# Five dense matmuls a slice instead of six, with a second partial sum in PSUM that is joined at eviction

## The chip, the cores and the metric

The kernel runs on one core of one Trainium2 chip. The metric is the device time of one execution in microseconds (us), median of several. TensorE (PE) multiplies, VectorE (DVE), ScalarE (ACT) and GpSimd (POOL) work elementwise, and SyncE (SP) issues the weight loads. Matmul results land in PSUM, eight banks of 512 fp32 columns per partition; all else that is on the chip lies in SBUF.

## The reference

One inference step of a two-layer recurrent decoder, in fp32, for one prompt of 512 tokens and eight sample sequences of 4 tokens, which share the weights: T = 544 tokens in all. D_MODEL is 2048. Cut to what matters:

```
layer 0: u = rmsnorm(h) @ ab_w_in     -> DeltaNet heads and GLA heads -> y
layer 1: u = rmsnorm(h) @ cd_w_in     -> SSD heads and RG-LRU channels -> y
h = h + y @ (ab_w_out | cd_w_out)
h = h + sigmoid(rmsnorm(h) @ ple_w_gate) * (p @ ple_w_proj)
```

Six large products with the 544 tokens: into `ab` (57 tiles of 128 output columns), `out0` (16), `gate0` (16), `cd` (37), `out1` (16), `gate1` (16), 158 tiles together.

## The kernel before, in words

Activations stand transposed: the 2048 model columns lie on 16 groups of 128 partitions, tokens along the free axis. A *slice* is one 128x128 block of weights times the 544 tokens; a *tile* is 16 slices, whose sum is 128 output columns for all tokens. There are 158 x 16 = 2528 slices.

To reach fp32 accuracy with the fp32r format each operand is split in two: x = xh + xl and w = w_hi + w_lo. A slice is three products, w_hi.xh, w_lo.xh and w_hi.xl, each over two halves of 272 tokens (`HALF`), since one matmul writes one PSUM bank: six matmuls of 272 columns (line 582). All three products add into the same columns. Each of them loads its stationary block first.

Weights come in *quarters* of four slices. SP loads a quarter into `w_raw` (six buffers), ACT copies it to `w_hi` (`split_hi`, line 1136), DVE subtracts to get `w_lo` (`split_lo`, line 1683), and PE waits for `lo_ready`. The dense tiles alternate between two PSUM buffers, `psd[0]` and `psd[1]`, of two banks each; tile d may begin when tile d-2 has been evicted (`dense_read`).

Between dense slices PE does the small *work groups* of the branches (into `psw`, also two buffers); a written plan (`target`, `FILL`, `LEAD`) says after which dense slice each group is issued. Each engine has a function `fill(to)` that does its share of the dense work up to slice `to`: on ACT the w_hi copies, on DVE the evictions and the w_lo subtractions. The branches' own steps on ACT and DVE stand between the calls of `fill`, in program order. A group waits for the reader of the group two before it and for its own inputs.

Evictions, all on DVE, each over 544 columns from `D0` = 240 on: for `ab` and `cd` tiles `evacuate(d)` multiplies by the row scale `rstd` (line 1708); in the `out` stages h is added (line 2350); in the `gate` stages line 2377 multiplies by `rstd`, ACT takes the sigmoid (1522), and DVE multiplies by the projection and adds into h (2388, 2390). At a stage's last tile (`last_tile`) ACT and DVE already make xh (`hi_part`, line 1205) and xl (`lo_part`, line 1745) for the next stage's *head* tile, whose slices wait for them one by one. POOL sums squares for the norm (line 2590), and PE adds them up over partitions in a norm group (lines 604 and 605).

## Time and profile before

| | |
|---|---|
| median of 3 runs | 2451.63 us (2447.52 to 2455.24) |
| span of the profiled execution, first to last instruction | 2447.1 us |
| the profiled execution's own time | not listed apart; the runs lie 0.4 to 8.1 us above the span |
| PE busy | 2384.2 us (97%), 21567 matmuls |
| dense matmuls (line 582) | 15168 of them |
| DVE / ACT / POOL busy | 52% / 39% / 15% |
| DMA | 111 GB/s on average |
| mean granted TensorE clock | 0.993 of full |

Matmuls overlap in the records: one of 272 columns is recorded with some 290 ns, but the next one starts 125 ns after it. For the cost of a matmul the distance from start to start is to be read, not the duration. The page's idle times are what is left when nothing of an engine is recorded as running.

### The profile page before, as it was taken

The numbers are of one execution on the slowest core, as the hardware profiler recorded it, in microseconds if no ns is written. First come the engines' busy times: TensorE is split into PE (matmuls) and PEld (weight loads), VectorE is DVE, ScalarE is ACT, GpSimd is POOL, SyncE is SP. The second block draws the span as 40 slices with busy tenths as digits, with TensorE's granted clock in tenths as the row PEclk, the third lists the DMA queues.
The fourth block names the chain that finished last, engine by engine and source line by source line (L and its number), as shares of the span: only waits on it lengthen the run. The fifth ranks groups of instructions, "written<-read, shape, count | busy, mean of one in ns | idle before, by whom it ended". The sixth has DMA issues, their size and how long they took to land.

```text
span 2447.1 us, 50327 instructions
## 1 busy us (share of the span) xinstructions
PE 2384.2 (97%) x21567; PEld 2273.9 (93%) x21567; DVE 1280.8 (52%) x2387; ACT 958.4 (39%) x1547; POOL 373.5 (15%) x558
## 2 busy tenths in 40 slices
PE   7999999999999999999999999999999999999996
PEld 7998999988999999899999999988899999999996
DVE  6655656565654564622444465566656663243432
ACT  5523444323444344432332353443355553243332
POOL 3101101111101101111111212122212211111111
PEclk9999999999999999999999999999999999999998
DMA  9433333333344454552233343233323354223232
GB/s 232 115 103 107 116 98 116 108 90 106 108 121 117 136 152 122 194 161 87 87 97 109 110 114 92 70 89 87 86 80 103 95 190 127 87 83 96 79 88 76
DMA packets 375535, 271.16 MB, mean 111 GB/s; under 512 B 24419, under 2 KB 346733, under 8 KB 374800
## 3 DMA queue, kind: packets, MB, share of 16 engines
q1 hardware_dynamic: 341424, 172.53, 26.0%
q0 software_dynamic: 22080, 72.77, 9.3%
q10 hardware_dynamic: 11808, 22.63, 2.6%
q8 instruction: 171, 2.80, 0.5%
q14 instruction: 52, 0.43, 0.1%
HBM read 220.24 MB, written 48.37 MB: 110 GB/s over the span
## 4 chain that ended last, share of the span: by engine, by line
PE 86%; DVE 6%; ACT 5%; issue 2%; DMA 1%; POOL 0%; ACTq 0%; DVEq 0%; POOLq 0%
PE psd L582 71%; PE psw L605 2%; PE psw L604 2%; PE psw L632 1%; PE psw L682 1%; DVE arena L1967 1%; PE psw L660 1%; PE psw L668 1%; ACT w_hi L1136 1%; DVE w_lo L1683 1%; PE psw L674 0%; PE psw L646 0%; PE psw L654 0%; PE psw L971 0%; PE psw L1066 0%
## 5 line engine op out<-in xcount | busy, mean ns | idle before, releaser
L582 PE MATMUL psd<-xh,w_hi 128*128 128x272 f32 x5056 | 1098.3, 298 | 8.9 <-DVE w_lo L1683 5.3
L582 PE MATMUL psd<-xl,w_hi 128*128 128x272 f32 x5056 | 1048.4, 289 | 2.9 <-DVE xl L1745 2.1
L582 PE MATMUL psd<-xh,w_lo 128*128 128x272 f32 x5056 | 1045.2, 288 | 0.0
L582 PEld LDWEIGHTS psd<-xh,w_hi 128*128 128x128 f32 x5056 | 795.0, 189 | 60.0 <-issue 40.5
L582 PEld LDWEIGHTS psd<-xh,w_lo 128*128 128x128 f32 x5056 | 796.4, 189 | 0.0
L582 PEld LDWEIGHTS psd<-xl,w_hi 128*128 128x128 f32 x5056 | 792.2, 189 | 4.2 <-DVE xl L1745 3.1
L1683 DVE TENSOR_TENSOR w_lo<-w_raw,w_hi 128x512 fp32r<-128x512 f32 x632 | 433.7, 706 | 380.5 <-ACT w_hi L1136 379.4
L1136 ACT CAST w_hi<-w_raw 128x512 fp32r<-128x512 f32 x632 | 376.7, 616 | 573.2 <-PE psd L582 499.3
L2590 POOL TENSOR_TENSOR states<-states,extra 128x544 f32<-128x544 f32 x59 | 86.7, 1469 | 514.4 <-ACT extra L1191 514.3
L2377 DVE TENSOR_TENSOR extra<-psd,rstd 128x544 f32<-128x544 f32 x32 | 23.2, 724 | 156.0 <-PE psd L582 138.9
L2350 DVE TENSOR_TENSOR arena<-arena,psd 128x544 f32<-128x544 f32 x32 | 23.1, 721 | 136.7 <-PE psd L582 129.9
L1792 DVE SCALAR_TENSOR_TENSOR arena<-raws,pv,arena 128x511 f32<-128x511 f32 (+2 forms) x120 | 86.2, 748 | 2.0
L1522 ACT ACTIVATE extra<-extra 128x544 f32<-128x544 f32 x32 | 21.1, 660 | 135.2 <-DVE extra L2377 135.2
L2512 POOL DMA_DIRECT2D raws<-uT_scratch x27 | 18.7, 692 | 347.8 <-DMA uT_scratch<-mix 323.0
L2525 POOL COPY smp<-hist 128x24 f32<-128x24 f32 x44 | 15.7, 357 | 277.5 <-DVE raws L1708 233.7
L1708 DVE TENSOR_TENSOR mix<-psd,rstd 128x544 f32<-128x544 f32 x55 | 39.3, 715 | 26.9 <-PE psd L582 23.5
L1708 DVE TENSOR_TENSOR raws<-psd,rstd 128x544 f32<-128x544 f32 x39 | 28.1, 721 | 43.0 <-PE psd L582 42.7
L605 PE MATMUL psw<-rawsR,mixR 128*128 128x288 f32 x192 | 49.4, 294 | 0.0
L604 PE MATMUL psw<-rawsR,mixR 128*128 128x256 f32 x192 | 48.9, 280 | 0.0
L1745 DVE SCALAR_TENSOR_TENSOR xl<-arena,pv,xh 128x544 fp32r<-128x544 f32 x64 | 45.9, 778 | 2.6 <-ACT xh L1205 2.5
L2618 POOL DMA_DIRECT2D raws<-in_ple_w_proj_dram x32 | 23.0, 720 | 158.1 <-DVE extra L2388 158.1
L1205 ACT ACTIVATE xh<-arena,pv 128x544 fp32r<-128x544 f32 x64 | 42.5, 739 | 6.6 <-DVE arena L2350 5.0
(514 smaller groups left out, 2376.9 us busy)
## 6 DMA issues: line engine op xcount, KB each, us to landing
w_raw<-in_ab_w_in_dram SPq DMA_DIRECT2D x224, 256.0 KB, 3.0
w_raw<-in_cd_w_in_dram SPq DMA_DIRECT2D x148, 256.0 KB, 3.0
w_raw<-in_ple_w_gate_dram SPq DMA_DIRECT2D x128, 256.0 KB, 3.1
w_raw<-in_ab_w_out_dram SPq DMA_DIRECT2D x64, 256.0 KB, 2.8
w_raw<-in_cd_w_out_dram SPq DMA_DIRECT2D x64, 256.0 KB, 2.8
uT_scratch<-mix ACTq DMA_DIRECT2D x53, 272.0 KB, 2.2
hT_scratch<-arena POOLq DMA_DIRECT2D x8, 1088.0 KB, 6.4
arena<-hT_scratch POOLq DMA_DIRECT2D x8, 1088.0 KB, 9.5
```

Of the source, the lines that this page charges most:

```text
L582: mm = pe.matmul(out[:, D0 + HALF * half:D0 + HALF * (half + 1)], w[:, r, k % QH, :], x[:, k, HALF * half:HALF * (half + 1)], start=(k == ...
L604: pe.matmul(W[:, SEQ - CUT:SEQ], lhsT, rhs[:, 0:CUT], **kw)
L605: return pe.matmul(W[:, SEQ:SEQ + T - CUT], lhsT, rhs[:, CUT:T], **kw)
L632: mm = pe.matmul(W[rows, c], lhsT(t, j), rhs[rows, c], start=True, stop=True)
L660: pe.transpose(W[:, P * t:P * t + P], src[:, P * t:P * t + P], ident[:, :])
L1136: act.copy(w_hi[:, q % NW], w_raw[:, q % NW]).then_inc(S["hi_ready"], 1)
L1205: act.mul(xh[:, c, :], hT(c), src[:, c:c + 1]).then_inc(S["x_hi"], 1)
L1683: dve.tensor_tensor(w_lo[:, q % NW], w_raw[:, q % NW], w_hi[:, q % NW].bitcast(F32), ALU.subtract).then_inc(S["lo_ready"], 1)
L1708: dve.tensor_tensor(dst, psd[d % 2][:, D0:D0 + T], rstd[:, :], ALU.mult)\
L1745: dve.scalar_tensor_tensor(xl[:, c, :], hT(c), src[:, c:c + 1], xh[:, c, :].bitcast(F32), ALU.mult, ALU.subtract).then_inc(S["x_ready"], 1)
L1792: go(dve.scalar_tensor_tensor(y, x, w, y, ALU.mult, ALU.add))
L2590: pool.tensor_tensor(acc, acc, extra[:, T * (2 + c % 2):T * (3 + c % 2)], ALU.add)\
```

## The change

The six matmuls of a slice become five. The first 288 tokens (`NA`) have three, w_hi.xh, w_lo.xh and w_hi.xl, in the tile's first bank. The other 256 (`NBK`) have two: one matmul of 512 columns with w_hi, whose moving operand is 256 columns of xh followed by the same 256 columns of xl, and one of 256 columns, w_lo.xh. The 512-column one fills the whole second bank with two sums: columns 512 to 767 hold w_hi.xh + w_lo.xh, columns 768 to 1023 hold w_hi.xl. To make that operand possible xh and xl become one tensor `xhl`, with a slice's xh row and xl row one behind the other.

At eviction the two sums are joined. For `ab`, `cd` and `gate` tiles (126 of them) ACT waits for the tile's end and copies the second sum to SBUF (`copy_low`, 128x256), and DVE adds it to the first in place (`join`) before it evicts as before. For the 32 `out` tiles DVE adds 544 columns into h and then, in a second instruction that waits for the first, the 256 of the second sum. At a head tile PE waits for `x_ready` after two matmuls of the slice instead of after four. `D0` is 224.

```diff
-        xh, xl = sb("xh", [P, KT, T], F32R), sb("xl", [P, KT, T], F32R)
+        xhl = sb("xhl", [P, KT, 2, T], F32R)
+        xh, xl = xhl[:, :, 0, :], xhl[:, :, 1, :]
...
-                out = psd[d % 2]
-                for i, (w, x) in enumerate(((w_hi, xh), (w_lo, xh), (w_hi, xl))):
-                    if head and i == 2:
-                        pe.wait_ge(S["x_ready"], KT * ph + k + 1)
-                    for half in range(2):
-                        mm = pe.matmul(out[:, D0 + HALF * half:D0 + HALF * (half + 1)], w[:, r, k % QH, :],
-                                       x[:, k, HALF * half:HALF * (half + 1)],
-                                       start=(k == 0 and i == 0), stop=(k == KT - 1 and i == 2))
-                mm.then_inc(S["slice_done"], 1)
+                hi, lo = w_hi[:, r, k % QH, :], w_lo[:, r, k % QH, :]
+                own, both = psd[d % 2][:, D0:SEQ], psd[d % 2][:, SEQ:2 * SEQ]
+                pe.matmul(own, hi, xhl[:, k, 0, 0:NA], start=k == 0, stop=False)
+                pe.matmul(own, lo, xhl[:, k, 0, 0:NA], start=False, stop=False)
+                if head:
+                    pe.wait_ge(S["x_ready"], KT * ph + k + 1)
+                pe.matmul(own, hi, xhl[:, k, 1, 0:NA], start=False, stop=k == KT - 1)
+                pe.matmul(both.rearrange("p (i t) -> p i t", i=2), hi, xhl[:, k, :, NA:T], start=k == 0, stop=False)
+                pe.matmul(both[:, 0:NBK], lo, xhl[:, k, 0, NA:T], start=False, stop=k == KT - 1)\
+                    .then_inc(S["slice_done"], 1)
...
+            def copy_low(d):
+
+                lows[0] = d + 1
+                if d in LOW:
+                    act.wait_ge(S["slice_done"], tile_end(d))
+                    if d >= 2:
+                        act.wait_ge(S[f"dense_read{d % 2}"], d // 2)
+                    act.copy(low[:, d % 2], psd[d % 2][:, SEQ + NBK:SEQ + 2 * NBK]).then_inc(S["low_copied"], 1)
... (ACT fill)
+                    if n % SL == 0 and lows[0] < n // SL:
+                        copy_low(n // SL - 1)
                     for q in SPLITS.get(n, []):
                         split_hi(q)
...
+                if to % SL == 0 and lows[0] < to // SL and TILES[to // SL - 1][3] in ("gate0", "gate1"):
+                    copy_low(to // SL - 1)
...
+            def join(d):
+
+                late = psd[d % 2][:, SEQ:2 * SEQ]
+                dve.wait_ge(S["slice_done"], tile_end(d))
+                dve.wait_ge(S["low_copied"], LOW[d] + 1)
+                link(dve.tensor_tensor(late[:, 0:NBK], late[:, 0:NBK], low[:, d % 2], ALU.add))
... (evacuate; the same in gate)
-                dve.wait_ge(S["slice_done"], tile_end(d))
+                join(d)
... (out_proj)
-                    dve.tensor_tensor(hT(c), hT(c), psd[d % 2][:, D0:D0 + T], ALU.add)\
+                    link(dve.tensor_tensor(hT(c), hT(c), psd[d % 2][:, D0:D0 + T], ALU.add))
+                    dve.tensor_tensor(hT(c)[:, NA:T], hT(c)[:, NA:T], psd[d % 2][:, SEQ + NBK:SEQ + 2 * NBK], ALU.add)\
                        .then_inc(S[f"dense_read{d % 2}"], 1)
```

## Rows read from the trace of the kernel before

**Rows 1.** The page's part 1, and PE and its granted clock in part 2
```profile
PE 2384.2 (97%) x21567; PEld 2273.9 (93%) x21567; DVE 1280.8 (52%) x2387; ACT 958.4 (39%) x1547; POOL 373.5 (15%) x558
...
PE   7999999999999999999999999999999999999996
...
PEclk9999999999999999999999999999999999999998
```

**Rows 2.** The page's part 4: the chain that ended last, by engine
```profile
PE 86%; DVE 6%; ACT 5%; issue 2%; DMA 1%; POOL 0%; ACTq 0%; DVEq 0%; POOLq 0%
```

**Rows 3.** PE's waits: waiting line, releaser: total us, places, longest; 25 rows
```profile
PE psw L1066 <- DMA ident<-in_cf_dram: 6.4, 1, 6.4
...
PE psw L610 <- ACT raws L1335: 0.2, 1, 0.2
```

**Rows 4.** PE's timeline in gate0: start us, us recorded, instruction, count
```profile
1364.79 0.41 PE L582 MATMUL psd<-xl,w_hi 128*128 128x272 f32 x2
...
1371.55 0.42 PE L582 MATMUL psd<-xl,w_hi 128*128 128x272 f32 x2
1371.80 0.28 PE L604 MATMUL psw<-rawsR,mixR 128*128 128x256 f32 x1
...
1373.28 0.41 PE L582 MATMUL psd<-xh,w_hi 128*128 128x272 f32 x2
```

**Rows 5.** Groups of PE by form: xcount | busy us, mean ns | idle before
```profile
L605 PE MATMUL psw<-rawsR,mixR 128*128 128x288 f32 x192 | 49.4, 294 | 0.0
L604 PE MATMUL psw<-rawsR,mixR 128*128 128x256 f32 x192 | 48.9, 280 | 0.0
...
L668 PE MATMUL psw<-states,arena 128*32 128x256 f32 x128 | 8.6, 385 | 0.0
...
L668 PE MATMUL psw<-states,arena 128*32 128x512 f32 x32 | 4.3, 604 | 0.0
```

**Rows 6.** Groups of DVE by form
```profile
L1683 DVE TENSOR_TENSOR w_lo<-w_raw,w_hi 128x512 fp32r<-128x512 f32 x632 | 433.7, 706 | 380.5 <-ACT w_hi L1136 379.4
...
L2350 DVE TENSOR_TENSOR arena<-arena,psd 128x544 f32<-128x544 f32 x32 | 23.1, 721 | 136.7 <-PE psd L582 129.9 <-DMA arena<-hT_scratch 6.8
...
L2124 DVE TENSOR_TENSOR arena<-raws,arena 128x256 f32<-128x256 f32 x20 | 8.3, 416 | 0.0
```

**Rows 7.** Groups of ACT by form: a copy of 256 columns out of PSUM
```profile
L1410 ACT COPY extra<-psw 128x256 f32<-128x256 f32 x8 | 3.0, 375 | 62.6 <-PE psw L668 62.6
```

**Rows 8.** All engines' waits: evictions of ab and cd tiles
```profile
DVE raws L1708 <- PE psd L582: 42.7, 18, 6.1
...
DVE mix L1708 <- PE psd L582: 23.5, 10, 4.7
```

**Rows 9.** The timeline at a tile's end in an ab stage, 407 to 412 us
```profile
411.01 1.12 ACT L1136 CAST w_hi<-w_raw 128x512 fp32r<-128x512 f32 x2
...
411.65 1.29 DVE L1683 TENSOR_TENSOR w_lo<-w_raw,w_hi 128x512 fp32r<-128x512 f32 x2 [3.17 <-ACT w_hi L1136]
```

**Rows 10.** The timeline from gate0 to cd
```profile
1436.90 4.59 ACT L1205 ACTIVATE xh<-arena,pv 128x544 fp32r<-128x544 f32 x7
...
1439.17 0.41 PE L582 MATMUL psd<-xl,w_hi 128*128 128x272 f32 x2
...
1439.70 4.95 DVE L1745 SCALAR_TENSOR_TENSOR xl<-arena,pv,xh 128x544 fp32r<-128x544 f32 x7
...
1444.57 0.71 DVE L2377 TENSOR_TENSOR extra<-psd,rstd 128x544 f32<-128x544 f32 x1
...
1448.97 1.48 POOL L2590 TENSOR_TENSOR states<-states,extra 128x544 f32<-128x544 f32 x1 [17.12 <-ACT extra L1191]
...
1452.21 0.59 PE L604 MATMUL psw<-states,ones 128*128 128x256 f32 x2
```

**Rows 11.** The timeline at the start of out0
```profile
1051.74 0.52 PE L582 MATMUL psd<-xh,w_hi 128*128 128x272 f32 x2 [3.14 <-DVE arena L2350]
```

**Rows 12.** The timeline behind the last dense slice
```profile
2419.02 0.72 DVE L2377 TENSOR_TENSOR extra<-psd,rstd 128x544 f32<-128x544 f32 x1 [10.31 <-PE psd L582]
```

More of the change, by code:

```diff
@@ L30 @@
 TAPS = 4
-HALF = T // 2
-D0 = SEQ - HALF
 CUT = SEQ // 2
+NA, NBK = T - CUT, CUT
+D0 = SEQ - NA
 WT = slice(SEQ - CUT, SEQ - CUT + T)
@@ L183 @@
 SEMS = """w_landed0 w_landed1 w_landed2 w_landed3 w_landed4 w_landed5 hi_ready lo_ready slice_done dense_read0 dense_read1 stage_stored0 stage_stored1
-act_chain dve_chain pool_chain work_ready in_copied nrm_sq nrm_ln nrm_rstd x_hi x_ready y_done h_loaded0 h_loaded1 h_loaded2 h_loaded3 z_loaded dn_z gl_z cd_z x_read sq_added sq_summed
+act_chain dve_chain pool_chain low_copied work_ready in_copied nrm_sq nrm_ln nrm_rstd x_hi x_ready y_done h_loaded0 h_loaded1 h_loaded2 h_loaded3 z_loaded dn_z gl_z cd_z x_read sq_added sq_summed
 consts_loaded params_loaded rows_loaded xy_loaded0 xy_loaded1 xy_loaded2 xy_loaded3 xy_loaded4 xy_loaded5 h_stored
@@ L259, in trunk @@
         wa2 = sb("wa2", [P, GLA_KW])
+        low = sb("low", [P, 2, NBK])
         C32 = c32[:, 0:6 * 32].rearrange("p (l j) -> p l j", l=6)
@@ L385, in trunk @@
         POS = {dk: n for n, dk in enumerate(ORDER)}
+        LOW = {d: i for i, d in enumerate(d for d, t in enumerate(TILES) if t[3] not in ("out0", "out1"))}
         def tile_end(d):
@@ L1123, in _ @@
         def _(act):
-            at, chained, stores, split, loaded = [0], [0], [0], [0, 0], [0, 0]
+            at, chained, stores, lows, split, loaded = [0], [0], [0], [0], [0, 0], [0, 0]
             def link(ins):
@@ L1154, in fill @@
                     at[0] += 1
+                if to % SL == 0 and lows[0] < to // SL and TILES[to // SL - 1][3] in ("gate0", "gate1"):
+                    copy_low(to // SL - 1)
+                if to in (end_slice("ab"), end_slice("cd")) and lows[0] < to // SL:
+                    copy_low(to // SL - 1)
                 if to in (end_slice("ab"), end_slice("cd")) and stores[0] < to // SL:
@@ L2368, in gate @@
                         last_tile(3)
-                    dve.wait_ge(S["slice_done"], SL * (d + 1))
+                    join(d)
                     if c == 0:
```

## The prediction

> **What bounds the kernel now.** I read the page's busy shares first, then the chain that ended last, then what PE waited for, then the timeline at the places which the change touches. PE is busy 97% of the span at a granted clock of nine tenths of full or more in every fortieth of the span but the last [rows 1]. The chain that sets the end runs 86% through PE [rows 2]. PE's whole list of waits has 25 rows; they add up to about 39.5 us in 53 places, 6.4 us of it at the very start [rows 3]. So PE's own stream is the bound, and DVE at 52% and ACT at 39% mostly follow it: of the idle time before DVE's w_lo subtractions 379 us end with ACT's w_hi [rows 6]. What counts is the distance from one dense matmul's start to the next.
>
> **The dense stream, the term that gains.** In gate0, 28 rows of two dense matmuls each run from 1364.79 to 1371.80 us, 56 matmuls in 7.01 us, 125.2 ns each [rows 4]. At 2.4 GHz, the upper of the clock's two levels, 272 columns take 113.3 ns. So 11.9 ns of a matmul are over its columns. The question is whether they are fixed per matmul or grow with the columns. Right behind stand twelve fp32r matmuls of 256 and 288 columns by turns: 1.48 us [rows 4] for 3264 columns, which are 1.36 us, so 10 ns each over. Their recorded durations are 280 ns for 256 columns and 294 ns for 288 [rows 5], 14 ns for 32 columns, or 0.44 ns a column; 1/2.4 is 0.417, and the whole distance spread over the columns would be 125.2/272 = 0.460. The row with 512 columns is an fp32 one: 604 ns against 385 for 256 [rows 5], 0.855 ns a column where two passes at full clock are 0.833. That is 2.6% over, not 10.5%. Most of the extra is thus fixed, and a matmul that fills a whole bank shows nothing else that is odd.
>
> The columns stay: 3 x 288 + 512 + 256 = 1632 = 6 x 272. A slice is now 6 x 125.2 = 751 ns, and will be 680 + 5 x 11.9 = 739.5 ns. That saves 11.9 ns x 2528 slices = 30.1 us. With the 10 ns of the mixed stream in the new slice (680 + 50 = 730 ns) it would save 21 ns a slice, 53 us; with the extra wholly proportional to columns, nothing. The 512-column matmul reads its operand as two runs of 256, one row of the tensor apart. No matmul in the trace has such an operand; from below it costs nothing, from above I allow as much as a matmul's whole extra, 12 ns a slice, which would eat the gain. I take nothing, since each of its runs is one of contiguous columns, as every operand in the trace is. So 30 us.
>
> A page of the Trainium skill speaks against so much. "TensorE: Matmul & The Clock Gate", section "Back-to-back issue gap", gives an isolated matmul's distance as the columns at 2.4 GHz and about 2.5 ns; by it the sixth matmul costs 6.3 us in all. The rows above show 10 to 12 ns over the columns where each matmul has its own weight load, so the measurement decides. The same section gives about 131 ns as the sustained distance at 512 columns with weight loads, below the 213 ns of the columns; by that the slice would lose another 94 ns.
>
> **Where the gain doesn't reach.** In the first fortieth of the span (61 us) PE is busy seven tenths, while x is brought in [rows 1]; at 751 ns that is room for 81 slices at most. The dense matmuls before a place where PE waits for a chain of DVE and ACT (I count 60 slices around the starts of out0 and out1) only make that wait longer. 141 x 11.9 ns = 1.7 us less. Total so far: -28.4 us.
>
> **DVE's and ACT's new work.** A join is a DVE tensor_tensor of 128x256. The nearest row has that shape in SBUF: 416 ns [rows 6]. The 544-column form with a PSUM operand is 721 ns [rows 6], 305 ns for 288 more columns, which fits a cost by the column, so writing back to PSUM should not be far off; bounds 0.35 to 0.55. I take 0.42, and 0.05 for the wait on its end. It comes 126 times, and the second `out` add 32 times: 158 x 0.42 = 66 us more of DVE, 52% to 55%. ACT's copy out of PSUM has a row of its size: 375 ns [rows 7], 126 of them, 47 us, 39% to 41%. Both stay far under PE's total. It is their place that matters.
>
> *ab and cd tiles (94).* The evicting DVE waited for PE in 28 of the 94 [rows 8]; in the other 66 it was late already. Where DVE is on time it now waits for ACT's copy (0.1 + 0.375), joins (0.47) and then evicts: 0.95 us later. Where it is late, 0.47. In a third case ACT is the later one, since `copy_low` stands in ACT's order where `split_hi` does: ACT comes to its w_hi copies at 411.01, and DVE, done with a tile's eviction at 411.65 - 3.17 = 408.48, waits for them till 411.65 [rows 9]. There the eviction itself moves behind 411.4, and the w_lo behind it by copy + join + eviction less the w_hi copy, about 1.0 us. What is queued behind on DVE are the w_lo subtraction, which PE needs four quarters (some 12 us) later, so it is covered, and the branch's next steps, for which a work group may wait. The next-but-one dense tile has 12 us of cover as well. On average 0.7 us of DVE delay per tile, 66 us in all, and PE sees of it only what goes beyond a group's slack. PE waits for such chains now in some 32 of its 53 places, with under 20 us [rows 3], mostly 0.2 to 1 us each, while the tables of the code hold over 400 groups: nearly all of them have slack. I take one tile in ten as exposed with 0.7 us, and the waits already there a little longer: +7 us. Bounds: 0, and 66 us.
>
> *gate0 to cd.* ACT makes seven xh parts from 1436.90 on, before the tile's end at about 1439.6 (the last two dense matmuls start at 1439.17), DVE the xl parts from 1439.70, then the eviction at 1444.57 [rows 10]. Now ACT's copy, which waits for the tile's end, stands before those seven: they start 3.1 us later, at 1440.0. DVE starts on them at 1440.8 instead of 1439.7 and is 1.1 us late, plus 0.47 for the join: 1.6. The norm's last sum on POOL ends at 1448.97 + 1.48 = 1450.45, and PE's norm group comes at 1452.21 [rows 10]: 1.8 us of cover, less 0.2 for the faster slices. +0 to 0.5, I take 0.2.
>
> *Start of out0 and out1.* PE waited 3.14 us for the first `out` eviction [rows 11], which itself had waited for h from DRAM [rows 6]. The second add comes before `dense_read`: +0.47, and the chain before it through the last branch is late by one eviction, 0.5. Twice: +1.9.
>
> *The end.* The last tile's eviction at 2419.02, for which DVE sat idle 10.31 us [rows 12], now has copy and join before it, and all that follows hangs on it: +0.95 us.
>
> **Sum.** -28.4 + 7 + 0.2 + 1.9 + 0.95 = -18.4 us in the middle estimate, with the fixed extra at its upper reading; with the 10 ns reading of the mixed stream given one chance in four, the stream's term becomes about -34 (0.75 x 28.4 + 0.25 x 51) and the sum -24. I take -24 us, on the span of 2447.1: 2423. What lies around the span, and the run-to-run difference, put the median of the runs 4.5 us above it (2451.6), so 2451.6 - 24 = 2427.6 us. A measurement of this kernel tells about 0.3%, 7.4 us, from no change.
>
> **Rivals.**
> *A, forecast:* the extra is fixed per matmul and the delays stay mostly hidden: 2427.6, its own range 2402 (730 ns a slice, nothing exposed but 3 us: -50) to 2443. Chance 0.76.
> *B, no change:* the extra goes with the columns, or the two-run operand costs what the sixth matmul did, or the exposures are 25 us. For it: the single distances of 256 and 288 columns can't be told from a proportional cost by their sum. Against it: the 14 ns between their durations and the 512-column fp32 row. Gain 0 to 12 less exposures of 5 to 10: 2448, chance 0.12. By the skill's isolated gap the time would be this one too.
> *C, slower:* the join makes each eviction wait for ACT, and the delay reaches PE through the work groups. Place: the 94 ab and cd tiles. Price: up to 1.0 us a tile. It decides from 28.4/94 = 0.30 us exposed per tile on. At 0.6 us: 56 - 28 + 3 = +31, 2482. For it: DVE is late at 66 of 94 evictions, so it has backlog in these stages. Against it: only some 32 of PE's places wait for such chains now. Chance 0.11.
> *D, much faster:* the 512-column matmul overlaps its neighbours and costs no more than one of 272 columns, 125 ns instead of 225: 100 ns x 2528 = 253 us on top, 2175. Nothing in the rows goes under one column a cycle; chance 0.01. The skill's sustained figure would be this case.
>
> Faster 0.76 + 0.01, less 0.02 for the part of A within 0.3%, and 0.02 from B: 0.77. Same 0.12. Slower 0.11. The range of 8 in 10 takes in A but for its lower tail, and B: 2408 to 2450.
>
> **What the profile after would show.** PE with 21567 - 2528 = 19039 matmuls. In a dense stretch a slice of 739 ns (730 to 740) from start to start of its first matmuls: 3 x 132, 225, 118.5. At 751 ns B is right about the stream. The sum of PE's waits at 45 to 55 us against 39.5 makes A's delays right; over 70, C. DVE's w_lo subtractions still with much idle time before them, and the join with a mean of 0.35 to 0.55 us. The gate0 to cd passage with the eviction some 1.6 us later against the tile's end, and PE's norm group not waiting over 0.5 us. The forecast fails if the 512-column matmul takes over 237 ns to the next start, or if PE's idle time grows by over 25 us.

## The result, and the profile after

The changed kernel takes 2472.01 us (median of 4 runs, 2469.34 to 2474.72) beside 2451.16 us of the kernel before on the same chip: ratio 1.0086, 95% interval 1.0072 to 1.01. It is 21 us slower where 24 us faster were forecast, and outside the range.

The page after, its parts 1, 2 and 4 (beside [rows 1, 2]):
```profile
span 2470.5 us, 45799 instructions
PE 2392.2 (97%) x19039; PEld 2148.4 (87%) x19039; DVE 1350.6 (55%) x2545; ACT 998.5 (40%) x1673; POOL 382.9 (15%) x558
...
PEclk9999999999999999999999999999999999999997
...
PE 81%; DVE 9%; ACT 5%; issue 2%; DMA 1%; POOL 0%; ACTq 0%; DVEq 0%; POOLq 0%
```
All 2528 matmuls are gone, and PE is busy 8 us longer. The clock looks as before at this grain; its mean is 0.989 in this execution, and 0.988 to 0.990 in the four, against 0.993 in the profiled one of before and 0.989 to 0.994 in all of its executions. Of the chain that ended last, PE holds 81% instead of 86%, DVE 9% instead of 6%. So two things are to be found: where the 30 us of the stream went, and what 21 us more is.

*The stream.* PE's timeline in gate0, a stretch of seven slices with nothing between them (start us, us recorded, instruction):
```profile
1369.77 0.29 PE L582 MATMUL psd<-xhl,w_hi 128*128 128x288 f32 x1
1369.90 0.29 PE L583 MATMUL psd<-xhl,w_lo 128*128 128x288 f32 x1
1370.03 0.29 PE L586 MATMUL psd<-xhl,w_hi 128*128 128x288 f32 x1
1370.17 0.39 PE L587 MATMUL psd<-xhl,w_hi 128*128 128x512 f32 x1
1370.40 0.28 PE L588 MATMUL psd<-xhl,w_lo 128*128 128x256 f32 x1
1370.52 0.29 PE L582 MATMUL psd<-xhl,w_hi 128*128 128x288 f32 x1
...
1375.04 0.28 PE L608 MATMUL psw<-rawsR,mixR 128*128 128x256 f32 x1
```
5.27 us for seven slices, 753 ns each, where 739.5 were forecast and six matmuls took 751 [rows 4]. Over all undisturbed slices of the two traces (the distances between the records' starts, averaged by position) it is 752.2 ns after and 751.9 before. The five distances are 133.9, 132.1, 133.4, 233.6 and 119.2 ns; forecast were 132 three times, 225 and 118.5. The 512-column matmul has 8 of the 13 ns that are too many.

*The delays.* Three rows of PE's waits; all 28 are 55.4 us in 69 places, against 39.3 in 53 before [rows 3]. The first was 3.1 us in 7 places before, the second 2.1 in 3, the third 1.4 in 2.
```profile
PE psw L664 <- DVE arena L2004: 4.8, 7, 1.4
PE psw L608 <- ACT arena L1298: 4.6, 6, 1.1
...
PE psw L650 <- DVE arena L2150: 2.6, 2, 1.8
```
Where they lie shows in busy time by stretch: most of the ab stage (60 to 1035 us) and of the cd stage (1480 to 2060). Columns: window, its length, then busy us and instructions of PE, PEld, DVE, ACT, POOL, then the granted clock, the DMA share and GB/s. First the kernel before:
```profile
60.00:1035.00 975.00, 964.91 (x10342) 892.40 (x10342) 563.64 (x1157) 385.91 (x585) 108.76 (x180) 1.00 0.41 119
...
1480.00:2060.00 580.00, 570.33 (x4519) 538.87 (x4518) 346.05 (x634) 256.23 (x422) 121.05 (x223) 1.00 0.36 102
```
and after:
```profile
60.00:1035.00 975.00, 951.12 (x9331) 827.26 (x9330) 578.34 (x1200) 397.52 (x633) 104.39 (x178) 1.00 0.40 116
...
1480.00:2060.00 580.00, 569.54 (x3873) 505.62 (x3872) 368.89 (x685) 267.48 (x462) 122.97 (x223) 1.00 0.37 103
```
PE idles 23.9 us instead of 10.1 in the ab stage (975 less its busy time), 10.5 instead of 9.7 in cd. The growth of the idle time is an affair of ab. It isn't all of the delay: over the two spans, 2447.1 and 2470.5 us, PE's idle time grows by 15.4 us and its busy time by 8.0, though the slices take as long as before.

One of the new waits, in both traces. Before, DVE and PE in the ab stage:
```profile
517.04 1.30 DVE L2002 STREAM_TRANSPOSE arena<-arena 32x128 f32<-32x128 f32 x4
518.37 0.72 DVE L1708 TENSOR_TENSOR mix<-psd,rstd 128x544 f32<-128x544 f32 x1
...
520.04 0.30 DVE L2005 COPY arena<-psw 32x128 f32<-32x128 f32 x1
520.49 0.31 PE L775 MATMUL psw<-arena 32*32 32x32 f32 x5
```
and the same place after, with ACT's copy:
```profile
525.82 1.31 DVE L2028 STREAM_TRANSPOSE arena<-arena 32x128 f32<-32x128 f32 x4
527.16 0.37 ACT L1149 COPY low<-psd 128x256 f32<-128x256 f32 x1 [8.27 <-PE psd L588]
527.64 0.43 DVE L1710 TENSOR_TENSOR psd<-psd,low 128x256 f32<-128x256 f32 x1 [0.51 <-ACT low L1149]
528.11 0.72 DVE L1734 TENSOR_TENSOR mix<-psd,rstd 128x544 f32<-128x544 f32 x1
...
529.77 0.30 DVE L2031 COPY arena<-psw 32x128 f32<-32x128 f32 x1
530.22 0.31 PE L779 MATMUL psw<-arena 32*32 32x32 f32 x5 [1.01 <-DVE arena L2031]
```
The tile ends as DVE comes to it. Before, the eviction starts 1.33 us after the transposes began; now 2.29, which is 0.96 us more: 0.51 waiting for ACT, 0.47 the join. The branch's small copies stand behind it, PE's work group behind them, and PE waits 1.01 us where it didn't.

The wait has a sequel, which is part of the 8 us of busy time. Busy time by stretch right behind it, before and after (the columns are those above; the third number from the end is the granted clock):
```profile
523.00:530.00 7.00, 7.00 (x69) 6.40 (x71) 1.44 (x3) 0.89 (x2) 2.38 (x12) 1.00 0.51 157
```
```profile
532.70:539.50 6.80, 6.80 (x34) 5.99 (x33) 1.44 (x3) 0.00 (x0) 2.27 (x11) 0.50 0.54 163
```
After the wait and a few groups of small matmuls the clock is at the lower of its two levels, 1.2 GHz, for 6.8 us; before, the same groups left it at 1.00. The same dense matmul of the passage starts at
```profile
527.49 0.50 PE L582 MATMUL psd<-xh,w_hi 128*128 128x272 f32 x2
```
```profile
540.19 0.38 PE L582 MATMUL psd<-xhl,w_hi 128*128 128x288 f32 x1
```
that is 7.00 us after the group of line 775 before, and 9.97 us after that of line 779 now: 3.0 us more, behind a wait of 1.0. The trace after has two more stretches at 0.50 or 0.51 that the one before hasn't, from 2014.0 and from 2239.3 us, 3.4 us each. Work at half the rate for these 13.6 us is, as an estimate, up to 6.8 of the 8 us. A part of it doesn't need the eviction: the kernel without it (e3, below) has one like the last, from 2220.6, and a longer one than before at the start of out0.

### The profile page after: what moved, and what is told of

It reads as the page before. It is cut to its first block, busy times and chain, and to the rows that moved or that the text cites. A ratio compares the mean times of both kernels' runs of the same rounds, so it can differ in the third digit from the quotient of the medians.

```text
span 2470.5 us, 45799 instructions
## 1 busy us (share of the span) xinstructions
PE 2392.2 (97%) x19039; PEld 2148.4 (87%) x19039; DVE 1350.6 (55%) x2545; ACT 998.5 (40%) x1673; POOL 382.9 (15%) x558
## 4 chain that ended last, share of the span: by engine, by line
PE 81%; DVE 9%; ACT 5%; issue 2%; DMA 1%; POOL 0%; ACTq 0%; DVEq 0%; POOLq 0%
PE psd L587 20%; PE psd L582 13%; PE psd L586 12%; PE psd L583 12%; PE psd L588 11%; PE psw L609 2%; PE psw L608 2%; DVE w_lo L1702 1%; PE psw L636 1%; PE psw L686 1%; DVE arena L1993 1%; PE psw L664 1%; DVE arena L1849 1%; ACT w_hi L1140 1%; PE psw L672 1%
## 5 line engine op out<-in xcount | busy, mean ns | idle before, releaser
L587 PE MATMUL psd<-xhl,w_hi 128*128 128x512 f32 x2528 | 1001.8, 396 | 0.0
L582 PE MATMUL psd<-xhl,w_hi 128*128 128x288 f32 x2528 | 800.1, 316 | 8.7 <-DVE w_lo L1702 5.5
L586 PE MATMUL psd<-xhl,w_hi 128*128 128x288 f32 x2528 | 750.6, 297 | 2.7 <-DVE xhl L1771 2.1
L583 PE MATMUL psd<-xhl,w_lo 128*128 128x288 f32 x2528 | 745.7, 295 | 0.0
L588 PE MATMUL psd<-xhl,w_lo 128*128 128x256 f32 x2528 | 714.7, 283 | 0.0
L582 PEld LDWEIGHTS psd<-xhl,w_hi 128*128 128x128 f32 x2528 | 477.1, 189 | 150.3 <-issue 40.0
L583 PEld LDWEIGHTS psd<-xhl,w_lo 128*128 128x128 f32 x2528 | 480.3, 190 | 2.7
L586 PEld LDWEIGHTS psd<-xhl,w_hi 128*128 128x128 f32 x2528 | 476.7, 189 | 4.8 <-DVE xhl L1771 3.3
L587 PEld LDWEIGHTS psd<-xhl,w_hi 128*128 128x128 f32 x2528 | 477.5, 189 | 0.0
L588 PEld LDWEIGHTS psd<-xhl,w_lo 128*128 128x128 f32 x2528 | 477.3, 189 | 0.0
L1710 DVE TENSOR_TENSOR psd<-psd,low 128x256 f32<-128x256 f32 x126 | 53.9, 428 | 260.9 <-ACT low L1149 255.2
L2617 POOL TENSOR_TENSOR states<-states,extra 128x544 f32<-128x544 f32 x59 | 93.8, 1591 | 506.5 <-ACT extra L1210 506.3
L1149 ACT COPY low<-psd 128x256 f32<-128x256 f32 x126 | 46.6, 370 | 293.7 <-PE psd L588 292.5
```

Source lines behind the costliest of these rows:

```text
L582: pe.matmul(own, hi, xhl[:, k, 0, 0:NA], start=k == 0, stop=False)
L583: pe.matmul(own, lo, xhl[:, k, 0, 0:NA], start=False, stop=False)
L586: pe.matmul(own, hi, xhl[:, k, 1, 0:NA], start=False, stop=k == KT - 1)
L587: pe.matmul(both.rearrange("p (i t) -> p i t", i=2), hi, xhl[:, k, :, NA:T], start=k == 0, stop=False)
L588: pe.matmul(both[:, 0:NBK], lo, xhl[:, k, 0, NA:T], start=False, stop=k == KT - 1)\
L1710: link(dve.tensor_tensor(late[:, 0:NBK], late[:, 0:NBK], low[:, d % 2], ALU.add))
```

## The experiments

### Distances of single forms

One kernel that runs 64 matmuls of each form in a row, with nothing beside them.
```diff
+ pe.matmul(ps[c % 2][:, 0:512], W[:, c, :], X[:, c, 0, 0:512], start=True, stop=True)                 # L261
+ pe.matmul(... .rearrange("p (i t) -> p i t", i=2), W[:, c, :], X[:, c, :, 288:544], ...)             # L265
+ # 288, 272, 256, 128, 384 columns: L269 to L285; bf16 with 512, 256, 128: L289 to L297
```


> A kernel of its own, which computes none of the reference: blocks of 64 back-to-back matmuls of one form each (fp32r with 512, 384, 288, 272, 256, 128 columns; 512 as two runs of 256; bf16 512, 256, 128; the same weights each time), then 24 slices of the new form and 24 of the old, on data of the inputs. What counts is the distance from start to start. Theory P (what a matmul takes over its columns at 2.4 GHz is proportional to the columns in this format, some 0.044 ns a column): 235 ns at 512 in both layouts, 177 at 384, 125 at 272, 118 at 256, and both mixes at 752 ns a slice. Theory F (fixed 12 ns per matmul, and the 512-column operand of two runs costs 8 ns more): 225 at 512 contiguous, 233 as two runs, 172 at 384, 118.6 at 256, 65 at 128. Theory N (the extra comes from the other engines' and DMA's traffic beside it): all forms within 3 ns of their columns, since nothing else runs here.

Rows by line: recorded ns (least, median, most), then the first and the last start, in us. The distance is the difference of the two, divided by 63.
```profile
L261 PE MATMUL ps<-X,W x64: 389/389/389, 39.0 to 53.3; 128*128 128x512 f32 x64
L265 PE MATMUL ps<-X,W x64: 388/395/398, 53.5 to 68.2; 128*128 128x512 f32 x64
L269 PE MATMUL ps<-X,W x64: 292/294/296, 68.4 to 76.7; 128*128 128x288 f32 x64
...
L277 PE MATMUL ps<-X,W x64: 278/283/283, 84.9 to 92.4; 128*128 128x256 f32 x64
L281 PE MATMUL ps<-X,W x64: 224/274/280, 92.5 to 99.5; 128*128 128x128 f32 x64
...
L297 PE MATMUL ps<-Xb,Wb x64: 219/219/219, 131.6 to 135.1; 128*128 128x128 bf16 x64
```
In fp32r: 226.7 ns for 512 columns, 174.2 for 384, 131.7 for 288, 125.3 for 272, 119.8 for 256, 110.9 for 128. From 256 columns on that is 11.7 to 14.2 ns over the columns at 2.4 GHz, and it doesn't grow with their number; no engine or DMA worked beside it. In a stream of one form the extra is thus nearly fixed, as A of the prediction has it. At 128 columns 111 ns for 53 is another bound, and in bf16 the distances are 216, 109.2 and 55.8 ns, 2.5 over the columns. The change's operand (L265) takes 233.3 instead of 226.7. But the two slices as they stand in the kernels take 753 ns each, the six as the five. So the loss is in PE alone.

The bf16 distances agree with the isolated gap, columns at 2.4 GHz and about 2.5 ns, of the Trainium skill's "TensorE: Matmul & The Clock Gate", section "Back-to-back issue gap"; the fp32r ones do not, and neither format shows its sustained 131 ns at 512 columns.

### Operand in one piece; six matmuls with two sums; no join

```diff
- pe.matmul(both.rearrange("p (i t) -> p i t", i=2), hi, xhl[:, k, :, NA:T], ...)
+ pe.matmul(both, hi, xhl[:, k].rearrange("p i t -> p (i t)")[:, NA:NA + 2 * NBK], ...)        # e1
+ pe.matmul(both[:, 0:NBK], hi, xhl[:, k, 0, NA:T], ...)                                       # e2, two
+ pe.matmul(both[:, NBK:2 * NBK], hi, xhl[:, k, 1, NA:T], ...)
```


> The changed kernel, but the 512-column matmul reads 512 adjacent columns (256 of xh and then the first 256 of xl, so the wrong tokens of xl go into the second sum); all else as in the changed kernel. Theory P (extra proportional to the columns): the matmul stays at 233 to 235 ns, the time at 2472. Theory F (the two-run operand is what costs the saved matmul back): 225 ns, 8 ns x 2528 = 20 us less, 2452.

2463.12 us, ratio to the kernel before 1.0041 (1.0029 to 1.0054). Slices of 748.6 ns, 3.6 less than the change's, which is the 9 us (3.6 x 2528). The 512-column matmul still takes 232.0. So the two runs cost 3.6 ns a slice, and 9 ns a slice are still missing.

> The matmul part of the change undone alone: six matmuls a slice (3 x 288, 3 x 256 columns), but the late tokens' w_hi.xl still goes into the second sum and is joined at eviction. Both theories on the stream expect a slice of some 752 ns. If the new eviction is what costs the 21 us, the time is that of the changed kernel, 2472 (2465 to 2478). If the five-matmul form itself stalls PE (fewer matmuls ahead of a wait, a 512-column one behind it), it is nearer to 2451.

2474.52 us, 1.0087 (1.0074 to 1.0101), slices of 752.2 ns. Six matmuls with the change's own operands and joins cost what the five cost. In this order of the operands neither fewer nor larger matmuls gain.

The third keeps the five matmuls and drops the copy, the join and the second `out` add:
```diff
-                if d in LOW:
+                if False:
-                dve.wait_ge(S["low_copied"], LOW[d] + 1)
-                link(dve.tensor_tensor(late[:, 0:NBK], late[:, 0:NBK], low[:, d % 2], ALU.add))
```


> The eviction part undone alone: five matmuls a slice as in the changed kernel, but no copy by ScalarE, no add by VectorE and no second add in the out stages; the second sum (w_hi.xl of the last 256 tokens) is left out of the results. If the 21 us are all the eviction's: 2451 (2446 to 2456), since the five-matmul slice takes 752 ns as the six-matmul one did. If the stream had gained after all and the gain is hidden behind delays: 2420 to 2440. If the five-matmul form stalls by itself: 2460 and more.

2451.39 us, 0.9997 (0.9988 to 1.0006), 752.2 ns a slice. This parts the result cleanly: the stream as built is worth 0 us within 2, the eviction costs all 21.

### Where an operand begins

> A kernel of its own, which computes none of the reference: 40 back-to-back fp32r matmuls of each form, on data of the inputs, then 20 slices each of five mixes. It asks what in the 512-column operand of two runs cost 233 ns where 512 columns from a row's start took 227. Theory R (two runs as such): any two-run pattern is at 233, also one whose runs touch; one run from any start is at 227. Theory A (where the operand begins): one run from column 288 or 544 is at 232, two runs from column 0 at 227. Theory M (the mix: a matmul that changes the PSUM bank costs some ns): all streams at 227, and the 512-column matmul at 232 in every mix, contiguous or not.

Forty matmuls of 512 columns each, in a row: from column 0 of a 1088-column row (L261), from 288 (L265), from 256 (L269); then two runs 512 apart from 0 (L293).
```profile
L261 PE MATMUL ps<-X,W x40: 389/389/389, 33.3 to 42.2; 128*128 128x512 f32 x40
L265 PE MATMUL ps<-X,W x40: 387/394/398, 42.4 to 51.5; 128*128 128x512 f32 x40
L269 PE MATMUL ps<-X,W x40: 389/389/395, 51.7 to 60.6; 128*128 128x512 f32 x40
...
L293 PE MATMUL ps<-X,W x40: 389/389/393, 106.9 to 115.8; 128*128 128x512 f32 x40
```
226.7, 233.2, 227.1, 226.8 ns, and from 544 it is 233.2. In such a stream it is not the two runs: an operand whose every run starts at a multiple of 256 bytes is fast, one with a run that starts 128 bytes off costs 6.5 ns more. At 288 columns the same is 131.5 against 133.3; 256 columns from 288 take 118.7 and lose nothing. In the change the third 288 starts at column 544 and the large operand at 288, both 128 bytes off. Five mixes of the change's forms, run behind the streams, take 743 or 747 ns a slice, and the start doesn't sort them: two that differ only in the weights of the second matmul lie 3.4 ns apart (746.7 and 743.3).

### Packed, without and with the eviction

A slice's row as [xl 256 | xh 256 | xh 288 | xl 288]: every operand but the last starts at a multiple of 256 bytes, the large one is one run. DVE writes xl in two pieces; the second sum lies in psd columns 0 to 255.
```diff
-        xhl = sb("xhl", [P, KT, 2, T], F32R)
+        xhl = sb("xhl", [P, KT, 2 * T], F32R)
+                pe.matmul(both, hi, xhl[:, k, 0:2 * NBK], start=k == 0, stop=False)
+                pe.matmul(both[:, NBK:2 * NBK], lo, xhl[:, k, NBK:2 * NBK], start=False, stop=k == KT - 1)
```


> Five matmuls without the eviction part, as before in that kernel (the second sum is left out), and the operands laid so that the 512 columns are one run that begins at a multiple of 256 bytes: per slice [xl 256 | xh 256 | xh 288 | xl 288], the 256 tokens of the double sum being the first ones now. VectorE writes xl in two pieces. If the place of the operand is what ate the saved matmul: a 512-column distance of 227 to 229 ns instead of 233, a slice of 740 to 744 ns instead of 752, so 8 to 12 ns x 2528 = 20 to 30 us less than with the layout of the change: 2421 to 2432. If something in the kernel's own mix holds it at 750: 2448 to 2452.

2447.9 us, 0.999 (0.9981 to 0.9998); 748.7 ns a slice, the 512-column one still 232.6. The same 3.5 ns as in e1, which had begun at an off column. So the rule of the start, sound in a stream of one form, doesn't tell what the matmul costs among others.

> The same layout with the whole eviction of the change, full results. 21 us on top of the kernel without the join: 2442 to 2453. If the shorter slices expose more of the chains, up to 2458.

2472.97, 1.0089 (1.0075 to 1.0104), slices of 748.6 ns. The 9 us of the faster slices are gone. PE's waits are 65.1 us instead of the change's 55.4, but in a profiled execution of 2479.01 us, 6 above the median, so how much went into them is not sure.

### The slice by itself, and its orders

> A kernel of its own, which computes none of the reference: the exact slices of the packed kernel, of the change and of the kernel before, 16 of each with nothing else running, then parts of the packed slice (512 columns alone, accumulating or not, w_hi alone, other orders), and at the end the packed and the changed slice beside a busy VectorE and ScalarE. In the packed kernel the 512 columns took 233 ns, though they are one run from a multiple of 256 bytes, which took 227 by itself. Theory S (the slice's own order of weights, banks and operands): 232 to 233 ns here too in the exact slice, and 227 in the stream of 512 alone. Theory T (the other engines' reads and writes): 227 to 228 in the exact slice when it is alone, and 232 to 233 beside VectorE and ScalarE.

Alone, the packed slice takes 748.5 ns, the change's and the one before 753.0 each. With DVE and ACT kept busy beside the packed one and the change's, on SBUF buffers of their own: 748.5 and 753.0 again, so this traffic costs PE nothing. The 512-column matmul among its like takes 226 to 227 ns, accumulating or not. With w_hi alone the slice takes 749. With the 512 pair before the third 288 it takes 743. So the order matters.

> A kernel of its own, which computes none of the reference: the packed slice of five matmuls in all its 24 cyclic orders, the slice of six in 120 orders with the packed operands (288 and 256 columns) and in 120 with those of the kernel before (2 x 272), 6 to 8 slices of each, nothing else running. One order of five took 742.5 ns where the kernel's order takes 748.5, the only difference being which matmul follows which. If the neighbours matter in general, the orders of five spread over 735 to 755 ns and those of six over 740 to 760, with some six below the 752 of the kernel before, which would be a gain that needs no second sum. If it was that one order's luck, nearly all lie within 3 ns.

All orders, eight or six slices each. A, B, C are the 288s (w_hi.xh, w_lo.xh, w_hi.xl), D the 512, E the 256. First-matmul starts of ABCDE, the kernel's order, and of ACEBD:
```profile
51.27 0.30 PE L271 MATMUL ps<-X,w_hi 128*128 128x288 f32 x1
...
56.52 0.29 PE L271 MATMUL ps<-X,w_hi 128*128 128x288 f32 x1
...
110.97 0.29 PE L371 MATMUL ps<-X,w_hi 128*128 128x288 f32 x1
...
116.16 0.29 PE L371 MATMUL ps<-X,w_hi 128*128 128x288 f32 x1
```
Seven slices in 5.25 us and in 5.19: 750 and 741 ns, or 749 and 740 when the distances are averaged without the first slice of a block, with the same five matmuls. Four orders give 740.0 to 740.5, and none is clearly slower than the kernel's. Six matmuls with the halves of 272 as before: 745.5 to 757 over 120 orders. What sorts them is only the pattern of the halves over the slice, not the weights: 0 1 0 1 0 1, which is the kernel before, 751.5 to 752 (12 orders), 0 1 1 0 1 0 a mean of 746.4, 0 0 0 1 1 1 a mean of 756.6. Six matmuls of 288 and 256 columns lie at 745 to 760, and there the pattern doesn't do it alone: the 12 orders of 0 1 0 1 1 0 (0 being the 288s) by themselves span 747 to 760. Six against five at their best is 745.5 against 740.0: what the sixth matmul costs is 5.5 ns, under half of the 11.9 that I took.

### Orders in the kernel

The kernel before, with nothing but its six matmuls in another order:
```diff
-                for i, (w, x) in enumerate(((w_hi, xh), (w_lo, xh), (w_hi, xl))):
+                hi, lo = (w_hi, xh), (w_lo, xh)
+                for i, ((w, x), half) in enumerate(((hi, 0), (hi, 1), (lo, 1), ((w_hi, xl), 0), ((w_hi, xl), 1), (lo, 0))):
```


> The kernel before with one edit: the six matmuls of a slice in another order (w_hi.xh first half, w_hi.xh second, w_lo.xh second, w_hi.xl first, w_hi.xl second, w_lo.xh first), so that the halves come as 0 1 1 0 1 0 instead of 0 1 0 1 0 1. Alone that slice took 745.5 ns against 752. If the order acts in the kernel as alone: 6.5 ns x 2528 = 16 us less, 2435 (2431 to 2440), faster than both kernels. If not: 2451.

2443.78 us, 0.9968 (0.9955 to 0.998): faster than both kernels. Three slices in gate0 of this run, the starts of the first and the third, 1.48 us apart:
```profile
1367.02 0.41 PE L582 MATMUL psd<-xh,w_hi 128*128 128x272 f32 x2
...
1368.50 0.41 PE L582 MATMUL psd<-xh,w_hi 128*128 128x272 f32 x2
```
These two take 740 ns each and are among the quick ones; single slices of the run lie between 739 and 754. Over the whole run a slice is 748.7 ns, 3.2 less than before, not the 6 of the slice alone.

For the packed five the 512 is moved before the third 288, with the eviction (e13) and without (e14):
```diff
+                pe.matmul(both, hi, xhl[:, k, 0:2 * NBK], start=k == 0, stop=False)
                 pe.matmul(own, hi, xhl[:, k, NBK + T:2 * T], start=False, stop=k == KT - 1)
-                pe.matmul(both, hi, xhl[:, k, 0:2 * NBK], start=k == 0, stop=False)
```


> The packed kernel of five matmuls with the whole eviction, and the 512-column matmul before the third 288-column one instead of behind it. Alone 740 ns against 748.5: 8.5 ns x 2528 = 21 us less than 2473: 2451 (2447 to 2457). If the shorter slice exposes more of VectorE's chains: up to 2462. If the order does nothing in the kernel: 2473.

2464.03, 1.0055 (1.0043 to 1.0068).

> The same without the eviction part (the second sum is left out): what the stream of five could give at most, 2448 - 21 = 2427 (2422 to 2432), which would be the gain that a fixed 12 ns per matmul promised. If the order does nothing in the kernel: 2448.

2437.2, 0.9944 (0.993 to 0.9957), 744.0 ns a slice in both. Five matmuls can thus be had 14 us faster than the kernel before, and the eviction takes back twice that (2464.03 - 2437.2 = 26.8). Against the six in their better order the five without eviction gain 6.6 us (2443.78 - 2437.2), so measured against them even a free eviction would have given about a quarter of the forecast. In both kernels 3 to 4 ns a slice more remain than in the slice alone. DVE's and ACT's traffic changed nothing in the two slices tried, neither of them in these orders; DMA's and the many operand addresses of a kernel were not tried.

### The eviction taken apart

Each has the change's five matmuls and lacks the second `out` add. Adds alone (DVE adds zeros, nobody copies), the copy alone (its operand lies in SBUF, nobody waits), and copy with wait but no add:
```diff
-                dve.wait_ge(S["low_copied"], LOW[d] + 1)                                          # not in e4
+                    act.copy(low[:, d % 2], ident[:, 0:1].broadcast_to([P, NBK]))...             # e5
-                link(dve.tensor_tensor(late[:, 0:NBK], late[:, 0:NBK], low[:, d % 2], ALU.add))   # not in e5, e11
```


> Five matmuls; VectorE's join at eviction stands, but adds zeros that were set once, and nobody copies the second sum nor waits for a copy; no second add in the out stages. The second sum is left out of the results. Theory W (the wait for ScalarE's copy is what costs): 2452 to 2456, since 126 adds of 0.43 us are mostly hidden. Theory V (VectorE's own extra 54 us costs): 2464 to 2470.

> Five matmuls; ScalarE waits for each ab, cd and gate tile's end and makes a copy of 128x256 from SBUF at the place of the change's copy, but VectorE neither waits for it nor adds; no second add in the out stages. The second sum is left out. Theory W: ScalarE tied to the tile's end costs a little by itself, 2453 to 2460; if its own place in ScalarE's order is what delays the work groups, 2465 and more. Theory V: 2451.

> The changed kernel without any add of the second sum (left out of the results), while ScalarE copies it and VectorE waits for the copy before it evicts, as in the change. With the copy but no waiter the time was that of before (2452), with the adds but no waiting 2460, with both and the wait 2470. If wait and adds add up: 2458 to 2463. If the wait costs only by the backlog that the adds make: 2452 to 2456.

The change without the second `out` add alone:
```diff
-                    dve.tensor_tensor(hT(c)[:, NA:T], hT(c)[:, NA:T], psd[d % 2][:, SEQ + NBK:SEQ + 2 * NBK], ALU.add)
```


> The changed kernel without the second add of the 32 out tiles alone (the second sum is left out there). The change cost 21 us, of which VectorE's adds at ab, cd and gate tiles were 9 and ScalarE's copies without a waiter 0. What is left, 12 us, is the out adds or VectorE's wait for ScalarE. Theory W (the wait): 2469 to 2471, 1 to 3 us less than the change. Theory O (the out adds): 2460 to 2463.

| kernel | median us | ratio (95%) | over no join, us | PE idle 60 to 1035, us |
|---|---|---|---|---|
| no copy, wait, add (e3) | 2451.39 | 0.9997 (0.9988-1.0006) | 0 | 10.7 |
| copy alone (e5) | 2451.89 | 1.0002 (0.9993-1.0011) | 0.5 | 11.9 |
| copy and wait (e11) | 2454.22 | 1.0014 (1.0005-1.0023) | 2.8 | 14.1 |
| adds alone (e4) | 2460.31 | 1.0034 (1.0022-1.0047) | 8.9 | 18.3 |
| copy, wait, adds (e7) | 2469.62 | 1.0076 (1.0064-1.0088) | 18.2 | 21.7 |
| and the second `out` adds (the change) | 2472.01 | 1.0086 (1.0072-1.01) | 20.6 | 23.9 |

The row of the ab stage behind the last column, of e3, and a stretch of e7's ab stage:
```profile
60.00:1035.00 975.00, 964.31 (x9447) 839.98 (x9446) 567.25 (x1156) 385.52 (x584) 107.17 (x179) 1.00 0.41 119
```
```profile
531.90:542.10 10.20, 10.20 (x51) 8.88 (x51) 2.21 (x6) 0.00 (x0) 3.96 (x13) 0.50 0.44 132
```
The copy is free. Wait and adds cost 2.8 and 8.9 apart and 18.2 together, 6.5 more than their sum, where each of the three is known to 2 or 3 us. PE's idle time in ab has no such surplus: 3.4 and 7.6 us over e3 apart, 11.0 together. What has it is the clock. In ab the kernel with both (e7) ran at 0.50 for 17.0 us, in the stretch shown and from 453.4 to 460.2; the one with the adds (e4) for 6.8; e11 and e3 not at all. At half the rate that is up to 8.5 and 3.4 us, an estimate of some 5 of the 6.5. It rests on one profiled execution of each, and that the longer gaps bring the clock down was not shown by an experiment of its own.

> The changed kernel, full results, but VectorE makes the copy of the second sum itself (0.3 to 0.4 us) right before the add, so it never waits for ScalarE at an eviction. Theory W (the wait costs): 2458 to 2466, faster than the change though VectorE works some 45 us more. Theory V (VectorE's load costs): 2485 to 2495, slower than the change.

Here DVE copies the second sum itself, so that nothing waits for ACT:
```diff
-                dve.wait_ge(S["low_copied"], LOW[d] + 1)
+                link(dve.tensor_copy(low[:, d % 2], late[:, NBK:2 * NBK]))
```
2480.53, 1.0107 (1.0088 to 1.0126), 8.5 us slower than the change. A DVE copy of 0.42 us at each of the 126 evictions is dearer here than the wait for ACT.

> As the packed kernel with the whole eviction, but an ab or cd tile's 288 columns with one sum are evicted before the wait for ScalarE's copy, and the 256 joined ones after it: one VectorE instruction more per tile (0.44 + 0.42 instead of 0.72), and the wait behind the first. Theory W (the wait is half of the eviction's price): 3 to 8 us less than the packed kernel. If VectorE's load is what counts: 2 to 6 us more.

Packed, with the 288 finished columns evicted first:
```diff
-                join(d)
+                dve.tensor_tensor(dst[:, NBK:T], psd[d % 2][:, SEQ:SEQ + NA], rstd[:, NBK:T], ALU.mult)
+                join(d)
+                dve.tensor_tensor(dst[:, 0:NBK], psd[d % 2][:, NBK:SEQ], rstd[:, 0:NBK], ALU.mult)
```
2472.76, 1.0086 (1.0072 to 1.0099), against 2472.97 for packed: nothing gained. If the wait is hidden, the second eviction instruction costs as much; the two were not parted.

## Why the prediction was wrong

*What bounds the kernel: right.* PE stayed the bound, at 97%.

*The dense stream, "680 + 5 x 11.9 = 739.5 ns", the step that failed.* The premise was nearly sound: in a stream of one form the extra is 11.7 to 14.2 ns and doesn't grow with the columns. The conclusion was not. I applied one extra, read from one slice pattern, to another pattern, and the slice stayed at 752.2 ns: the term of -28.4 us was worth 0 (2451.39 without the eviction, against 2451.63). The rows had a hint of it. The twelve matmuls of 256 and 288 columns by turns in [rows 4] had 10 ns over their columns, and streams of each form by itself have 13.1 and 11.7; I took the 10 for another constant. Two things were left out. "I take nothing" for the operand: it costs 3.5 ns a slice in the kernel (752.2 to 748.7 and 748.6) and 4.5 alone. And the order of the operands within a slice, which no step named, is worth 9 ns (749 to 740). Together they are the 13 ns that the slice was too long. With both put right the slice alone takes 740.0 ns, which meets the 739.5 forecast, by chance in part: the sum had neither effect in it. In the kernel it takes 744.0, and 4.5 of the 13 ns stay unexplained. And the six matmuls profit from a better order as well, so the sixth was never worth 11.9 ns: 5.5 alone (745.5 to 740.0), 4.7 in the kernels (748.7 to 744.0). Why the order and the operand matter stays open. The bound of 12 ns for the operand, "which would eat the gain", was the right size for the sum of both; I should have weighed it, having written that no row shows such an operand.

*Where the gain doesn't reach, 1.7 us:* void, there was none.

*DVE's and ACT's new work: right.* The page's groups after, count, busy us, mean ns, idle before:
```profile
L1702 DVE TENSOR_TENSOR w_lo<-w_raw,w_hi 128x512 fp32r<-128x512 f32 x632 | 431.8, 704 | 312.4 <-ACT w_hi L1140 311.1
...
L1710 DVE TENSOR_TENSOR psd<-psd,low 128x256 f32<-128x256 f32 x126 | 53.9, 428 | 260.9 <-ACT low L1149 255.2
...
L1149 ACT COPY low<-psd 128x256 f32<-128x256 f32 x126 | 46.6, 370 | 293.7 <-PE psd L588 292.5
```
428 ns for 0.42, 370 for 375; the idle time ahead of w_lo fell from 381 [rows 6] to 312 us and is still large. That idle time proves nothing for the branches: DVE has much of it and yet is late at the work groups.

*ab and cd tiles, "one tile in ten as exposed": mis-sized.* The price per tile was right: 0.96 us at the place shown, 0.95 forecast. Exposed it was far oftener in ab, where PE's idle time grew by 13.8 us, 0.24 a tile over its 57 tiles, and hardly in cd (0.8 us). About 14.6 us of idle time stand for the 7. The sum had no term for the clock, though "granted clock of nine tenths" was its first reading: the stretch at 1.2 GHz in ab cost some 3 us more. I counted how many of PE's groups waited before; what counts is how many had under 1 us of slack, and the list of waits shows only those with none.

*gate0 to cd: right.*
```profile
1456.36 0.37 ACT L1149 COPY low<-psd 128x256 f32<-128x256 f32 x1 [1.69 <-PE psd L588]
...
1462.75 0.72 DVE L2404 TENSOR_TENSOR extra<-psd,rstd 128x544 f32<-128x544 f32 x1
...
1468.92 0.60 PE L608 MATMUL psw<-states,ones 128*128 128x256 f32 x2
```
The eviction comes 6.4 us after the tile's end (just before the copy's start) instead of 5.0 [rows 10], 1.4 later for the 1.6 forecast, and PE's norm group doesn't wait.

*Start of out0 and out1, 1.9 us: the size right, the reason not.* The second adds cost 2.4 us (2469.62 to 2472.01; the intervals of the two overlap), but the wait of [rows 11] didn't grow by 0.95:
```profile
1068.14 0.40 PE L582 MATMUL psd<-xhl,w_hi 128*128 128x288 f32 x1 [3.20 <-DVE arena L2377]
```
3.20 us for 3.14. Where the 2.4 lie is open.

*The end, 0.95 us: the step right, and more behind it.*
```profile
2440.61 0.38 ACT L1149 COPY low<-psd 128x256 f32<-128x256 f32 x1 [2.28 <-PE psd L588]
2441.09 0.43 DVE L1710 TENSOR_TENSOR psd<-psd,low 128x256 f32<-128x256 f32 x1 [9.88 <-ACT low L1149]
2441.56 0.72 DVE L2404 TENSOR_TENSOR extra<-psd,rstd 128x544 f32<-128x544 f32 x1
```
The eviction starts 0.95 us after the copy, as forecast. From it to the span's end are 28.9 us, 28.1 before [rows 12]: together 1.8, of which 0.9 were not looked for.

*The rivals.* B was right on the stream, with the sign it named (751 ns), and its second reason, the operand, is part of the cause. C's mechanism is what made the kernel slower: 18.2 us without the `out` adds are 0.19 us per ab or cd tile, under its point of 0.30, but that point stood on a gain of 28.4 us that didn't exist. I gave the two a chance each and none to both at once, though they have nothing to do with each other: 2448 and some 20 us of delays is near the measured time. The signs were too lax for it: the 512-column matmul took 233.6 ns, under the 237 named, PE's idle time grew by 15.4 us, under 25, and its waits are 55.4 us, hardly over the 45 to 55 that were to make A's delays right. Only the slice's 751 ns spoke. The sum's 24 us of gain leaned on one number, and the range should have held that number's failure together with the delays.

## What to carry to other kernels

The distance between matmuls belongs to the pattern that they stand in: measure the new slice by itself, in all its orders, before anything is built around it, since here a better order alone gave 7 us where the removed matmul gave none. Where PE is the bound, try an operand in one run (3.5 ns a slice here, in the kernel whether it started at a multiple of 256 bytes or not) and other orders. An instruction put ahead of evictions is to be priced by the groups with less slack than its length, which a list of waits doesn't show. Look at the granted clock behind the new gaps too: here one of 1.0 us was followed by 6.8 us at half the clock, which is three times the gap's price.

## What the runs showed of the hardware

- In a stream of one form an fp32r matmul with its own weight load takes 11.7 to 14.2 ns over its columns from 256 columns on; in bf16 2.5 ns. In the kernel the 288s take 132 to 134 ns and the 512 of two runs 233.6, 20 over. At 128 columns it takes 111 ns in fp32r. The same weights each time (227 ns) change nothing.
- In a stream an fp32r operand of 512 columns costs 226.7 ns from a multiple of 256 bytes and 233.2 from 128 bytes beside it, and a second run of columns costs nothing by itself (226.8). Inside the kernel's slice this doesn't hold: 232.0 from an off start, 232.6 from a multiple.
- The same five matmuls take 740 to 749 ns, the same six 745.5 to 757, by their order in the slice; with six of 272 columns it is which half of the columns follows which that sets the level. What in the chip does this, these runs can't tell: operand address and PSUM bank change together with the half.
- DVE and ACT at work on SBUF beside a stream don't change its distances (748.5 and 753.0 ns both ways).
- PE's clock can fall to 1.2 GHz inside a kernel that is 97% PE: 6.8 us at 0.50 right behind a wait of 1.0 us and groups of small matmuls, at a place where it stayed at 1.00 without the wait. The passage took 9.97 us instead of 7.00.
